# Two packed 64-row diagonal blocks in the inverse of the delta rule

## The reference, cut to what matters

```python
lmat = jnp.where(strict, jnp.einsum('bhnik,bhnjk->bhnij', kb, k) * decay, 0.0)
tmat = lax.linalg.triangular_solve(lmat + eye, jnp.broadcast_to(eye, lmat.shape),
                                   left_side=True, lower=True, unit_diagonal=True)
u = jnp.einsum('bhnij,bhnjd->bhnid', tmat, vb)
w = jnp.einsum('bhnij,bhnjd->bhnid', tmat, kb * jnp.exp(gc)[..., None])
```

## Time and profile before

| | us |
|---|---|
| median of 3 runs | 2421.75 (2419.52 to 2428.88) |
| the profiled execution | 2422.73 |
| its span, first to last instruction | 2420.9 |
| PE busy | 1971.5 (81%) |
| DVE busy | 1634.7 (68%) |
| ACT busy | 804.6 (33%) |
| mean granted TensorE clock | 0.909 of 2.4 GHz |

### The profile page before, as it was taken

One profiled execution on the slowest core, in us unless ns is written; L12 is line 12 of the kernel. 1 busy time (PEld: TensorE's weight loads), 2 busy tenths in 40 slices (PEclk: granted clock), 3 DMA queues, 4 the chain that ended last, 5 costly groups with the idle time before them and its releaser, 6 DMA issues. The chain is left out here.

```text
span 2420.9 us, 31905 instructions
## 1 busy us (share of the span) xinstructions
PE 1971.5 (81%) x11960; PEld 1291.7 (53%) x11960; DVE 1634.7 (68%) x3745; ACT 804.6 (33%) x1826; POOL 662.1 (27%) x657
## 2 busy tenths in 40 slices
PE   4998987688786689978869887895878884999898
PEld 3887886655341146545426554651434332868674
DVE  5668877478978577555476867658898544368863
ACT  3112222133333342553243455234423224233322
POOL 2222110044344433443243334333434330000000
PEclk9998998899897799999979998896899997899999
DMA  8997763199999999999989989999999994222200
GB/s 333 367 363 292 269 229 112 36 385 419 375 402 421 421 415 418 415 418 397 386 350 395 361 292 369 349 395 376 343 420 419 419 419 177 100 72 78 95 10 27
DMA packets 124684, 746.76 MB, mean 308 GB/s; under 512 B 13537, under 2 KB 16481, under 8 KB 56305
## 3 DMA queue, kind: packets, MB, share of 16 engines
q0 software_dynamic: 93792, 610.66, 63.2%
q1 hardware_dynamic: 30736, 134.05, 14.5%
HBM read 741.25 MB, written 3.41 MB: 308 GB/s over the span
## 5 line engine op out<-in xcount | busy, mean ns | idle before, releaser
L1787 POOL DMA_INDIRECT got<-in_peer_uv,idx x512 | 587.0, 1147 | 948.7 <-PE ps L1757 800.4
L1757 PE MATMUL ps<-got,diag 64*64 64x512 f32 x3936 | 596.8, 693 | 287.3 <-ACT diag L1844 269.7
L1884 DVE CUSTOM_DVE_ANT_0 got<-got,xk 128x1024 f32<-128x1024 f32 x512 | 616.6, 1222 | 260.4 <-DMA got<-in_peer_uv,idx 255.4
L1757 PEld LDWEIGHTS ps<-got,diag 64*64 64x64 f32 x3936 | 118.6, 145 | 560.2 <-ACT diag L1844 465.0
L1839 ACT ACTIVATE gelu<-eye,hid 128x64 f32<-128x64 f32 x492 | 169.9, 345 | 669.9 <-DVE hid L1884 668.5
L1331 PE MATMUL ps<-xT,ring 128*128 128x256 f32 x928 | 231.4, 397 | 0.0
L1331 PEld LDWEIGHTS ps<-xT,ring 128*128 128x128 f32 x928 | 174.0, 196 | 74.6 <-issue 47.3
L1027 PE MATMUL ps<-xT,ring 128*128 128x256 f32 x768 | 189.4, 396 | 1.8 <-ACT xT L1140 1.8
L1844 ACT ACTIVATE diag<-gelu,gate 128x64 f32<-128x64 f32 x492 | 171.0, 348 | 51.5 <-PE ps L1757 5.8
L1027 PEld LDWEIGHTS ps<-xT,ring 128*128 128x128 f32 x768 | 143.7, 194 | 75.7 <-issue 45.5
L192 POOL DMA_DIRECT2D vring<-in_vslabs x136 | 72.3, 532 | 276.9 <-DVE in_b_psums L304 140.1
(11 more groups left out here) (582 smaller groups left out, 2531.4 us busy)
## 6 DMA issues: line engine op xcount, KB each, us to landing
ring<-in_small SPq DMA_DIRECT2D x158, 512.0 KB, 7.9
vring<-in_vslabs POOLq DMA_DIRECT2D x136, 512.0 KB, 6.4
ring<-in_slabs SPq DMA_DIRECT2D x18, 2048.0 KB, 10.8
got<-in_peer_uv,idx POOLq DMA_INDIRECT x512, 13.1
h<-in_x SPq DMA_DIRECT2D x2, 2048.0 KB, 11.3
w_out<-in_slabs SPq DMA_DIRECT2D x2, 2048.0 KB, 10.5
out<-h SPq DMA_DIRECT2D x4, 512.0 KB, 2.6
bias_rows<-brow POOLq DMA_DIRECT2D x1, 1280.0 KB, 4.7
```

What stands on the lines that cost most here:

```text
L1757: mm = nc.tensor.matmul(ps[to:to + HALF, i, :], diag[own, d % NDIAG, :], got[own, n % GRING, 1, 512 * g:512 * g + 512], start=(k == 0), st ...
L1787: nc.gpsimd.indirect_dma_start(out=got[:, n % GRING].rearrange("p a d -> p (a d)"), out_offset=None, in_=table, in_offset=bass.IndirectOff ...
L1884: nc.vector.tensor_tensor_reduce(row_in, row_in, xk[:, w % 2, :], 1.0, 0.0, ALU.mult, ALU.add, hid[:, w % 2, k:k + 1]).then_inc(dotted, 1)
```

## The change

Of each head's matrices, levels 0 to 5 fill only the two diagonal blocks of 64x64. These are now kept packed: a tile of 128 partitions x 4 heads x 64, block 0 in partitions 0 to 63 and block 1 in partitions 64 to 127. `in_blocks` multiplies them with eight matmuls of 64x64x64 for four heads, block 0 in the quarter of rows and columns 0 to 63 of the array and block 1 in the opposite one, into the same bank. Level 6, which couples the two blocks, is four matmuls of 64x64x64 in one quarter for y (`across`), four for z. DVE and ACT work on 256 elements a partition instead of 512 in levels 0 to 5. LA makes the blocks and the coupling part of L in three operations on 64 partitions; step y of level 6 gains a memset and two copies that unpack `xt`; level 6 needs no mask, and step z of level 6 writes one block of `xt`. EYE is eight matmuls with a 64x64 identity instead of four transposes. The masks in `levels` shrink to 64 columns.

```diff
+            def in_blocks(b, lhs, rhs):
+                for a in range(HA):
+                    for own in HALVES:
+                        mm = nc.tensor.matmul(packed(t, b)[own, a, :], lhs[own, a, :], rhs[own, a, :], start=True, stop=True)
+                return mm
+
+            def across(b, to, frm, lhs, rhs):
+                for a in range(HA):
+                    mm = nc.tensor.matmul(packed(t, b)[to, a, :], lhs[frm, a, :], rhs[frm, a, :], start=True, stop=True)
                 return mm
...
             elif k == EYE:
-                pe.wait_ge(sg["c"], L * u + 1)
-                turn(2, tl["ct"]).then_inc(sg["y"], 1)
+                pe.wait_ge(sg["c"], (L - 1) * u + 1)
+                for a in range(HA):
+                    for own in HALVES:
+                        mm = nc.tensor.matmul(packed(t, 2)[own, a, :], tl["cs"][0][own, a, :], ident[own, own], start=True, stop=True)
+                mm.then_inc(sg["y"], 1)
...
-                pe.wait_ge(sg["c"], L * u + n + 1)
                 pe.wait_ge(sg["x"], (L - 1) * u + n)
-                heads(1, tl["cs"][n % 2], tl["xn"]).then_inc(sg["y"], 1)
+                if n < L - 1:
+                    pe.wait_ge(sg["c"], (L - 1) * u + n + 1)
+                    in_blocks(1, tl["cs"][n % 2], tl["xnb"]).then_inc(sg["y"], 1)
+                else:
+                    across(1, second, first_half, tl["lt"][:, :, second], tl["xnb"]).then_inc(sg["y"], 1)
...
                 if n < L - 1:
-                    heads(2, tl["xt"], tl["yc"]).then_inc(sg["za"], 1)
-                heads(0, tl["yc"], tl["xt"]).then_inc(sg["zb"], 1)
+                    in_blocks(2, tl["xtb"], tl["ycb"]).then_inc(sg["za"], 1)
+                    in_blocks(0, tl["ycb"], tl["xtb"]).then_inc(sg["zb"], 1)
+                else:
+                    across(0, first_half, second, tl["ycb"], tl["xtb"]).then_inc(sg["zb"], 1)
...
-                nc.scalar.activation(tl["yc"], bank(t, 1), ACT.Copy).then_inc(sg["yc"], 1)
+                made = slice(0, P) if n < L - 1 else second
+                nc.scalar.activation(tl["ycb"][made], packed(t, 1)[made], ACT.Copy).then_inc(sg["yc"], 1)
...
-                step(ve.tensor_tensor(tl["lt"], bank(t, 1), tl["decay"], ALU.mult))
-                ve.tensor_tensor(tl["ct"], tl["lt"], lev(0), ALU.mult).then_inc(sg["c"], 1)
-                dve.wait_ge(sg["c"], L * u + 1)
-                step(ve.tensor_tensor(tl["xt"], eye, tl["ct"], ALU.subtract))
+                for own in HALVES:
+                    step(ve.tensor_tensor(tl["lb"][own], bank(t, 1)[own, :, own], tl["decay"][own, :, own], ALU.mult),
+                         but=0 if own == second else 1)
+                ve.tensor_tensor(tl["lt"][first_half, :, second], bank(t, 1)[first_half, :, second],
+                                 tl["decay"][first_half, :, second], ALU.mult)
+                ve.tensor_tensor(tl["cs"][0], tl["lb"], lev(0), ALU.mult).then_inc(sg["c"], 1)
+                dve.wait_ge(sg["c"], (L - 1) * u + 1)
+                step(ve.tensor_tensor(tl["xtb"], eye, tl["cs"][0], ALU.subtract))
...
-                if n < L - 1:
-                    ve.tensor_tensor(tl["cs"][(n + 1) % 2], tl["lt"], lev(n + 1), ALU.mult).then_inc(sg["c"], 1)
+                if n < L - 2:
+                    ve.tensor_tensor(tl["cs"][(n + 1) % 2], tl["lb"], lev(n + 1), ALU.mult).then_inc(sg["c"], 1)
+                elif n == L - 1:
+                    ve.memset(tl["xt"][second, :, first_half], 0.0)
+                    dve.wait_ge(sg["xs"], (L - 1) * u + n - 1)
+                    for own in HALVES:
+                        ve.tensor_copy(tl["xt"][own, :, own], tl["xtb"][own])
...
-                    ve.tensor_tensor(tl["xn"], tl["xn"], bank(t, 2), ALU.subtract).then_inc(sg["x"], 1)
+                    ve.tensor_tensor(tl["xnb"], tl["xnb"], packed(t, 2), ALU.subtract).then_inc(sg["x"], 1)
                 dve.wait_ge(sg["zb"], (L - 1) * u + n)
-                if n > 1:
-                    dve.wait_ge(sg["xs"], (L - 1) * u + n - 1)
-                ve.tensor_tensor(tl["xt"], tl["xt"], bank(t, 0), ALU.subtract).then_inc(sg["xs"], 1)
+                if n == L - 1:
+                    ve.tensor_scalar(tl["xt"][first_half, :, second], packed(t, 0)[first_half], -1.0, None, ALU.mult).then_inc(sg["xs"], 1)
+                else:
+                    if n > 1:
+                        dve.wait_ge(sg["xs"], (L - 1) * u + n - 1)
+                    ve.tensor_tensor(tl["xtb"], tl["xtb"], packed(t, 0), ALU.subtract).then_inc(sg["xs"], 1)
```

More of the change, by code:

```diff
@@ L1916, in second_block @@
             w_uv = sbuf(st, "w_uv", [P, HB, P])
-            levels = sbuf(st, "levels", [P, LEVELS, P])
+            levels = sbuf(st, "levels", [P, LEVELS, HALF])
             state = sbuf(st, "dl_state", [P, HA, P])
@@ L1924, in build, with blocks @@
     by_head = lambda x: x.rearrange("p (h x) -> p h x", h=HA)
+    HALVES = [slice(HALF * i, HALF * i + HALF) for i in range(2)]
+    def blocks(x, i=0):
+        return by_head(x.rearrange("p h x -> p (h x)")[:, HA * HALF * i:HA * HALF * (i + 1)])
     def delta_set(st, tag, tiles):
@@ L1931, in delta_set @@
         tl |= {"qn": tl["lt"], "kn": tl["at"], "o": tl["vb"], "wT": tl["kbg"], "yc": tl["knT"], "vn": tl["knT"],
-               "low": tl["decay"], "cs": [tl["ct"], tl["kbT"]]}
+               "low": tl["decay"], "cs": [blocks(tl["ct"], 0), blocks(tl["ct"], 1)], "lb": blocks(tl["kbT"]),
+               "xnb": blocks(tl["xn"], 0), "xtb": blocks(tl["xn"], 1), "ycb": blocks(tl["knT"])}
         tl["ss"] = sbuf(st, f"dl{tag}_ss", [P, 2, HA])[:]
@@ L1959, in delta_tiles @@
         mine = lambda t: (sets[slot_of[t]], sigs[slot_of[t]], turn_of[t])
-        lev = lambda n: levels[:, n, :].unsqueeze(1).broadcast_to([P, HA, P])
-        eye = ident.unsqueeze(1).broadcast_to([P, HA, P])
+        lev = lambda n: levels[:, n, :].unsqueeze(1).broadcast_to([P, HA, HALF])
+        eye = lev(L - 1)
+        packed = lambda t, b: blocks(bank(t, b))
+        first_half, second = HALVES
         def w_before(t):
@@ L2123, in dve_step @@
                 dve.wait_ge(levels_loaded, 16)
-                step(ve.tensor_tensor(tl["lt"], bank(t, 1), tl["decay"], ALU.mult))
-                ve.tensor_tensor(tl["ct"], tl["lt"], lev(0), ALU.mult).then_inc(sg["c"], 1)
-                dve.wait_ge(sg["c"], L * u + 1)
-                step(ve.tensor_tensor(tl["xt"], eye, tl["ct"], ALU.subtract))
+                for own in HALVES:
[6 more added lines that the diff above has]
+                step(ve.tensor_tensor(tl["xtb"], eye, tl["cs"][0], ALU.subtract))
             elif k == EYE:
                 dve.wait_ge(sg["y"], L * u + 1)
-                ve.tensor_tensor(tl["xn"], eye, bank(t, 2), ALU.subtract).then_inc(sg["x"], 1)
-                ve.tensor_tensor(tl["cs"][1], tl["lt"], lev(1), ALU.mult).then_inc(sg["c"], 1)
+                ve.tensor_tensor(tl["xnb"], eye, packed(t, 2), ALU.subtract).then_inc(sg["x"], 1)
+                ve.tensor_tensor(tl["cs"][1], tl["lb"], lev(1), ALU.mult).then_inc(sg["c"], 1)
                 dve.wait_ge(sg["la"], 2 * u + 2)
@@ L2959, in shape_constants @@
     levels = []
-    for k in range(LEVELS):
+    q, x = p % HALF, f[:, 0:HALF]
+    for k in range(LEVELS - 1):
         b = 1 << k
-        levels.append((p // (2 * b) == f // (2 * b)) & (p // b % 2 == 0) & (f // b % 2 == 1))
+        levels.append((q // (2 * b) == x // (2 * b)) & (q // b % 2 == 0) & (x // b % 2 == 1))
+    levels.append(q == x)
     dist = np.maximum(T - 1 - np.arange(ZR), 0)
```

## The result

| kernel | median, us | runs, us |
|---|---|---|
| before | 2422.60 | 2418.54 to 2428.88, 8 runs |
| changed | 2408.82 | 2403.84 to 2416.38, 8 runs |

The account below looks back on a forecast made before the run. PE bounds tile 0, PE then DVE tile 1, and PE with DVE partly full tiles 2 and 3. -3.2 - 4.0 - 7.6 = -14.8 us takes 2422.7 to 2407.9, median forecast 2407.0; own range 2401 to 2413, full range 2400 to 2424.

Parts of the forecast that it names:

- a group of 16 records: On PE, eight 64x64x64 matmuls with both quarters together take 0.47 us; upper bound 0.93.
- into and out of the small shape, around a side job: On PE, small matmuls standing between whole-array work cost about 0.34 us extra (0.19 + 0.16).
- DVE, 256 columns: A DVE operation on 256 elements takes 0.42 us, against 0.68 on 512.
- tile 0 (A): Delta rule of token tile 0, from EYE to DU: PE alone bounds, -3.2 us.
- tile 1 (B): Delta rule of token tile 1, EYE to DW: PE bounds up to z of level 3, then DVE; -4.0 us.
- tiles 2 and 3 (C): Stretch from row tile 0's first output projection to before DU of tile 3: -7.6 us after stalls.
- rival 1: PE's instructions come too slowly; at 0.70 us a group the gain is 3.7 us, total 2418; chance 0.15.
- rival 2: The two quarters take turns, for the shared bank or otherwise: 0.93 us a group, +12.3 us, 2434; chance 0.13.
- The net on PE: Tiles 2 and 3: -14.2 us for groups, +4.1 for 12 changes of shape, net -10.1.
- The 1.0: Tiles 2 and 3: 1.0 us (0 to 3) lost to ACT's copy between y and z and DVE's lumps.
- Rival 3: Change of shape costs half of 0.34 us, next weights loading under the tail; total 2402; chance 0.08.
- Rival 4: Small matmuls with gaps lower the clock in tiles 2 and 3 for 10 us, costing about 5; 2412; chance 0.04.

Follow-up runs that it names:

- narrow_dve: Kernel before, with DVE's subtractions and masks and ACT's copy of y in the levels on 64 of each head's 128 columns; 2424.97 us, one run.
- wide_dve: Changed kernel, with each xn and xt subtraction and mask product in levels 1 to 5 done a second time into an unread tile; 2417.95 us, one run.
- one_quarter: Changed kernel, with block 0 computed twice in its quarter and block 1 left out in levels 1 to 5, same instruction count; 2424.65 us, one run.
- lump_later: Changed kernel, with DVE's last output-projection step of row tile 0 moved from program step 14 to 19; 2405.46 us, ratio 0.9907 to the kernel before.
- shape_between: Changed kernel, with one 128x128 single-column matmul between the two groups of each z in levels 1 to 5; 2420.51 us, one run.
- the changed kernel, again: Second measurement of the changed kernel, nothing altered; 2407.93 us, ratio 0.9922 to the kernel before.
- both: Changed kernel with the edits of lump_later and pool_masks together; 2406.68 us, ratio 0.9922 to the kernel before.
- pool_masks: Changed kernel, with the mask products of levels 2 to 5 of tiles 1 to 3 on GpSimd instead of DVE; 2409.96 us, ratio 0.9929 to the kernel before.

## Why the prediction was right

The forecast was 2407.0; the median is 2408.82, inside its own range of 2401 to 2413, and the whole is faster by over 0.5%.

| term | forecast | measured |
|---|---|---|
| a group of 16 records | 0.47 | 0.47 |
| into and out of the small shape, around a side job | 0.34 | 0.14 + 0.20 |
| DVE, 256 columns | 0.42 | 0.42 |
| tile 0 (A) | -3.2 | -3.5, -2.2, -2.4 |
| tile 1 (B) | -4.0 | -3.6 |
| tiles 2 and 3 (C) | -7.6 | -7.7, -8.6, -8.6 |

**A group on PE.** Taking it from L1757, a row of the same kind of array use, was the step that decided, and 0.47 is what came. The range up to 0.93 was open for two reasons, and both are settled. For rival 1, instructions too slow, 32 instructions come in 0.47 us over a whole z and over several groups in a row: 15 ns each, or 29 ns for each of the 16 MATMULs. The Trainium skill, "TensorE: Matmul & The Clock Gate", in its part on the 56 ns, gives about 62 ns of sequencer time for a MATMUL when hardware decode is off; the trace shows no such floor. For rival 2, quarters that take turns, the case that no row showed is now shown: two quarters with different rows, into different partitions of one bank, run together, and the same instructions in a single quarter take 0.93. The Trainium skill, "TensorEngine Tiling (Array Packing)", Gotcha 1: PSUM Pressure, says that different row tiles can't access the same PSUM bank at the same time. That does not hold for this case (0.47 instead of 0.93); the measurement decides.

**Tile 0.** -3.5 in the execution that had the clock back at nearly the same point as before. From y to the side job behind z a level's sum was 0.89 + 1.78 + 1.73 = 4.40 and became 0.61 + 1.08 + 1.93 = 3.62; with the 0.2 that the next side job costs more, this is the 0.6 of the prediction. Where the clock came back 2 to 3 us later, 1.1 to 1.3 of it is lost again.

**Tile 1.** DVE's work fell by 4.3 us (43.92 to 39.64) and the stretch by 3.6. That DVE ends last there, so that its saving counts and not PE's, is what narrow_dve (-2.9), wide_dve (+3.4) and one_quarter (-0.7 in spite of slow groups) show. The memset and the two copies take 0.27 + 0.59 us by the timeline, where 0.7 was put.

The sum for this tile, -4.0, came out better than its parts, and that is luck. It was made of 1.7 on PE up to z of level 3 and 2.3 on DVE from there on. PE did gain 2.0 by that z (24.95 to 22.95 us from EYE). But directly behind it PE waits for DVE's `dl_g` in both kernels, so this gain counts mostly because DVE gets there earlier as well: wide_dve, with PE's gain alone, keeps 0.2 of the whole stretch. From y of level 4 on the stretch became shorter by 1.3 us (20.32 to 19.03), not by 2.3. DVE's saving in levels 1 and 2, which the prediction did not count, belongs in the first part: narrow_dve, with PE's work of before, has y of level 4 begin 28.5 us after EYE instead of 29.8.

**Tiles 2 and 3.** The net on PE was put at -10.1 and idle time at +2.5 (1.5 where DVE bounds, 1.0 between y and z). At the full clock PE's work fell by 11.3 (73.40 to 62.15) and its idle time rose by 2.6 (1.23 to 3.87). So the waits were right in size, but only in part in kind: all four waits are for DVE (0.76, 0.25, 1.95 and 0.90 us), and none is for ACT's copy between y and z, which came to light only in lump_later, when DVE's lump was gone. The 1.0 had two reasons, ACT's copy and DVE's lumps, and only the second came. PE's work fell by 1.2 more than forecast, which would be 0.25 instead of 0.34 for each of the 12 changes of shape, the size that shape_between shows. No run takes the 12 apart.

**The mis-sized steps.** Rival 2's sum of +12.3 was wrong, though its group of 0.93 was right: one_quarter gives +3.6 - 0.7 + 0.7 = +3.6. It leaves EYE's four groups fast, which the rival's sum made slow as well, by 0.46 each, so some 2 us more may belong to it (an estimate). Even so this rival would not have been slower by 0.5%. Two terms failed. In B it took PE's full level as the new bound (+3.5), but PE had 5.3 us of idle time to spend first. In C it put PE's work at +4.6, where it rose by 1.9: the changes of shape cost 1.2 less, and the groups 13.1 more than in the changed kernel (62.15 to 75.28) instead of 14.7, in part because 30 of them were slowed and not 32. And it forgot 1.2 us of idle time. Rival 3 (shape at half its price) is out around the side jobs: 0.34. In C, with 0.25, it was half right. Rival 4, the clock in tiles 2 and 3, came true in a small form, 0.9 us in one of three profiles instead of 5. What the clock cost in A, 1.1 to 1.3 us in two of three profiles, no part of the prediction had.

## What to carry to other kernels

Small matmuls in opposite quarters of the array cost the time of one quarter, 0.47 us for eight records in each, if the quarters alternate in the order of issue; the sum is groups at that price plus about a third of a microsecond for every piece that stands between matmuls of another shape, so keep such pieces together. Before adding up what PE saves or loses, set its idle time and the second engine's work beside it for each stretch: a saving on PE and one on DVE were worth 7.7 to 8.6 us together here in C, where PE's alone was worth 4.0 and DVE's alone 1.4.

## What the hardware showed that was not expected

- Alternating the quarters matters: 0.47 us a group when alternated, about 0.75 when one quarter's eight records follow the other's, 0.93 in one quarter.
- The clock fell to 1.2 GHz for a few us behind the same wait of 1.95 us in C in one of three executions, and in B of the same execution behind a wait of 1.66 us that the other two have as well (1.69 and 1.67). At EYE of tile 0, with PE busy all along, it came back at two different points. These are the first two stretches of 3 us of A in the changed kernel, again, at 1.2 GHz in both:

```profile
2078.44:2081.44 3.00, 3.00 (x26) 2.88 (x26) 1.76 (x4) 0.77 (x2) 0.00 (x0) 0.50 0.14 57
2081.44:2084.44 3.00, 3.00 (x26) 2.66 (x26) 0.53 (x2) 0.07 (x1) 0.00 (x0) 0.50 0.00 0
```

By the granted clock of stretches of 1.5 us it came back 3.0 us after the start of A in all three executions of before, and 3.3, 6.2 and 5.6 us after it in those of the changed kernel. narrow_dve, made from the kernel before, had it back after 2.9 us; of the kernels made from the changed one, wide_dve and both had it back after 3.1 and 3.0, lump_later and pool_masks after 6.2. Whether the change brings the later point is open.
